# Weighted sums of eight decay heads: the value's high and low halves side by side in one weight block

## The reference, cut to what matters

```python
logit[t, s] = q_t . k_s / 8 + c[t] - c[s]          # c = cumulative sum of log forget gates, s <= t
p = softmax(logit)
attn = einsum('bhqk,bkhd->bqhd', p, v)              # per head: (512 x 512) x (512 x 64)
sgu = zu * (w_s @ layer_norm(zv) + b_s)             # z = gelu(...), split into zu, zv
merged = concat([rms_norm(attn), rms_norm(sgu)])
x = x + merged @ w_out
```

## Time and profile before

| | us |
|---|---|
| median of 3 runs | 1293.28 (1293.07 to 1293.45) |
| the profiled execution's own time | 1292.43 |
| its span | 1290.7 |
| PE busy | 1282.1 (99%) |
| DVE busy | 912.7 (71%) |
| ACT busy | 611.1 (47%) |
| POOL busy | 467.4 (36%) |

### The profile page before, as it was taken

How to read it: one execution, slowest core, us unless ns; L and a number is a source line. 1 busy time by engine, 2 the same in 40 slices (tenths; PEclk the granted TensorE clock), 3 DMA queues, 4 the chain that set the end, 5 groups by cost and what they waited for, 6 DMA issues and landing times.

```text
span 1290.7 us, 18190 instructions
## 1 busy us (share of the span) xinstructions
PE 1282.1 (99%) x6986; PEld 1095.9 (85%) x6986; DVE 912.7 (71%) x1284; ACT 611.1 (47%) x1007; POOL 467.4 (36%) x208
## 2 busy tenths in 40 slices
PE   9999999999999999999999999999999999999998
PEld 7787888898888888888889888898879999998886
DVE  7999826799283366666498685577989999985442
ACT  5223323335352466656654445578564444453223
POOL 2544544555434442452555343324420000015441
PEclk9999999999999999999999999999999999999999
DMA  4333333233832422326143346442323233223331
GB/s 165 98 98 106 116 96 99 66 98 115 293 97 83 133 64 82 83 63 216 49 147 115 116 152 167 124 115 99 98 69 128 99 110 120 99 94 103 114 98 66
DMA packets 48019, 143.66 MB, mean 111 GB/s; under 512 B 6048, under 2 KB 6048, under 8 KB 47040
## 3 DMA queue, kind: packets, MB, share of 16 engines
q1 hardware_dynamic: 43984, 129.88, 32.5%
q10 hardware_dynamic: 3952, 12.64, 2.7%
HBM read 121.46 MB, written 10.49 MB: 102 GB/s over the span
## 4 chain that ended last, share of the span: by engine, by line
PE 95%; DVE 2%; ACT 1%; issue 1%; DMA 0%; POOL 0%; SPq 0%; POOLq 0%; ACTq 0%
PE bank L2151 30%; PE bank L2153 30%; PE bank L2152 30%; PE bank L2389 2%; PE bank L2378 1%; PE bank L2379 1%; DMA x<-x_in 0%; POOL w_lo L714 0%; PE bank L2532 0%; PE bank L2533 0%; ACT pool_xg L822 0%; DVE zv L1884 0%; PE bank L2706 0%; ACT f_prob_t L1016 0%; DVE zu L1851 0%
## 5 line engine op out<-in xcount | busy, mean ns | idle before, releaser
L714 POOL TENSOR_TENSOR w_lo<-raw,w_hi 128x1024 fp32r<-128x1024 f32 (+1 forms) x146 | 372.8, 2558 | 518.6 <-ACT w_hi L782 518.5
L782 ACT ACTIVATE w_hi<-raw 128x1024 fp32r<-128x1024 f32 x149 | 156.1, 1053 | 176.1 <-PE bank L2153 93.5
L759 POOL TENSOR_TENSOR w_lo<-raw,w_hi 128x1024 fp32r<-128x1024 f32 x22 | 53.8, 2449 | 262.9 <-DVE w_lo L2008 204.5
L2151 PE MATMUL bank<-pool_xg,w_hi 128*128 128x512 f32 x248 | 98.6, 398 | 0.2 <-POOL w_lo L714 0.2
L2152 PE MATMUL bank<-pool_xg,w_hi 128*128 128x512 f32 x248 | 98.1, 396 | 0.0
L2153 PE MATMUL bank<-pool_xg,w_lo 128*128 128x512 f32 x248 | 98.1, 395 | 0.0
L2151 PE MATMUL bank<-right,w_hi 128*128 128x256 f32 x336 | 94.4, 281 | 0.0
L2153 PE MATMUL bank<-right,w_lo 128*128 128x256 f32 x336 | 94.1, 280 | 0.0
L2152 PE MATMUL bank<-right,w_hi 128*128 128x256 f32 x336 | 94.0, 280 | 0.0
L2090 DVE TENSOR_TENSOR act<-acts,act 128x512 fp32r<-128x512 f32 x22 | 47.6, 2167 | 51.0 <-ACT act L1249 51.0
L2151 PE MATMUL bank<-y_hi,w_hi 128*128 128x512 f32 (+1 forms) x216 | 81.0, 375 | 0.0
(11 more groups left out here) (469 smaller groups left out, 3726.2 us busy)
## 6 DMA issues: line engine op xcount, KB each, us to landing
raw<-stream SPq DMA_DIRECT2D x187, 512.0 KB, 3.5
raw_x<-stream SPq DMA_DIRECT2D x18, 512.0 KB, 4.7
xg_spill<-mla_xg ACTq DMA_DIRECT2D x2, 2048.0 KB, 12.0
rope_q<-turned_hl SPq DMA_DIRECT2D x64, 64.0 KB, 2.5
zx<-xg_spill SPq DMA_DIRECT2D x2, 1536.0 KB, 9.3
stacked<-fq SPq DMA_DIRECT2D x24, 128.0 KB
stacked<-fk SPq DMA_DIRECT2D x24, 128.0 KB
x<-x_in SPq DMA_DIRECT2D x4, 512.0 KB, 6.4
```

The source lines that it names most:

```text
L714: pool.tensor_tensor(w_lo[:, j % RING, 0:width], raw[:, j % RAW, 0:width], plain(w_hi[:, j % RING, 0:width]), ALU.subtract).then_inc(tile_ ...
L759: pool.tensor_tensor(w_lo[:, s, 0:D], raw[:, d % RAW, 0:D], plain(w_hi[:, s, 0:D]), ALU.subtract).then_inc(tile_lo, 1)
L782: act.activation(w_hi[:, t % RING, 0:width], raw[:, t % RAW, 0:width], ACT.Copy).then_inc(tile_hi, 1)
L2151: pe.matmul(target, a_hi, b_hi, start=start, stop=False)
```

## The change

It does five things.

1. The values are stored as `fv[P, NB, head, 2, 64]`: for every head the 64 high columns and the 64 low columns form one weight block of 128. A weighted sum is then two matmuls per key block (times the high and the low part of the probabilities) where three stood. Rows 0 to 63 of bank 5 hold the high values' sum, rows 64 to 127 the low values' sum.
2. ACT copies rows 64 to 127 to `low_half` for every head (`copy_low_half`), and DVE adds rows 0 to 63 of the bank to it, where it copied 64 rows before.
3. ACT's list in the heads is changed: casts of weight tiles 20, 21, 22, 23 stand in heads 4, 5, 7, 7 (before 4, 4, 5, 7); `attn_high(1)` is in head 5 instead of 4; the last evacuation of z is in two halves (`last_gates`), of which one goes to the end of head 5; the fourth `zvn_hi` goes to head 6. DVE's `attn_low(1)` goes from head 4 to the end of head 5.
4. PE counts `gates_halved` after the first fill of head 5.
5. DVE's scaling of a bank in `add_attention` counts `attn_taken`, and PE's branch transposes and later products wait for that instead of for the addition to x.

```diff
@@ values
-        fv_hi, fv_lo = (place(48 + 8 * i, f"fv_{i}", [P, NB, D_ATTN], f32r) for i in range(2))
+        fv = place(48, "fv", [P, NB, FOX_HEADS, 2, FOX_D], f32r)
+        low_half = place(155, "low_half", [FOX_D, S])
@@ ACT
+            def last_gates(part):
+                if part == 0:
+                    act.wait_ge(gates_halved, GATES_BEFORE + 1)
+                else:
+                    act.wait_ge(tile_used, MIXED["z", 7] + 1)
+                for b in range(2 * part, 2 * part + 2):
+                    act.activation(zu[:, b, QUARTER:], bank[6 + b // 2][:, QUARTER * (b % 2):QUARTER * (b % 2 + 1)], ACT.Copy,
+                                   scale=inv_t[:, b:b + 1]).then_inc(z_evac, 1)
+            def copy_low_half(h):
+                act.wait_ge(fox.weighted, h + 1)
+                if h:
+                    act.wait_ge(fox.out, h)
+                act.activation(low_half[:], bank[5][FOX_D:P, :], ACT.Copy).then_inc(low_half_copied, 1)
...
-                for i in ((12, 13), (14, 15), (16, 17), (18, 19), (20, 21), (22,), (), (23,))[h]:
+                for i in ((12, 13), (14, 15), (16, 17), (18, 19), (20,), (21,), (), (22, 23))[h]:
                     split_mix(i)
@@ DVE
-                if h in (2, 4):
-                    attn_low(h // 2 - 1)
+                if h == 2:
+                    attn_low(0)
+                if h == 5:
+                    attn_low(1)
                 dve.wait_ge(fox.weighted, h + 1)
-                dve.tensor_copy(attn[rows, h // 2, :], bank[5][rows, :]).then_inc(fox.out, 1)
+                dve.wait_ge(low_half_copied, HALVES_BEFORE + h + 1)
+                dve.tensor_tensor(attn[rows, h // 2, :], bank[5][0:FOX_D, :], low_half[:], ALU.add).then_inc(fox.out, 1)
@@ PE
-                    last = three(bank[5][:, P * b:S], fv_hi[:, b, a], fv_lo[:, b, a], f_prob_t_hi[:, r], f_prob_t_lo[:, r],
-                                 b == 0, b == NB - 1)
+                    v = fv[:, b, h, :, :].rearrange("p a d -> p (a d)")
+                    pe.matmul(bank[5][:, P * b:S], v, f_prob_t_hi[:, r], start=b == 0, stop=False)
+                    last = pe.matmul(bank[5][:, P * b:S], v, f_prob_t_lo[:, r], start=False, stop=b == NB - 1)
...
-                    pe.wait_ge(attn_added, 2)
+                    pe.wait_ge(attn_taken, TAKEN_ATTN + 2)
```

More of the change, by code:

```diff
@@ L460, in build @@
         v_summed, fv_hi_done, fv_lo_done = sem("v_summed"), sem("fv_hi_done"), sem("fv_lo_done")
+        low_half_copied, HALVES_BEFORE = lat_mean, 2
+        gates_halved, GATES_BEFORE = rope_k_summed, 1
+        attn_taken, TAKEN_ATTN = lat_inv, 2
         gate_abs_ready, gate_log, log_f_ready = sem("gate_abs_ready"), sem("gate_log"), sem("log_f_ready")
@@ L1123, in _ @@
                     act.wait_ge(v_summed, b + 1)
-                act.activation(fv_hi[:, b, :], bank[V_BANK[b]][:], ACT.Copy, scale=inv_t[:, b:b + 1]).then_inc(fv_hi_done, 1)
+                act.activation(fv[:, b, :, 0, :], by_head(bank[V_BANK[b]][:]), ACT.Copy, scale=inv_t[:, b:b + 1]).then_inc(fv_hi_done, 1)
             split_mix(11)
@@ L1136, in attn_square, with zvn_high @@
                 act.activation(attn_sq[:, pair, :], attn[:, pair, :], ACT.Square).then_inc(attn_squared, 1)
+            def zvn_high(b):
+                act.wait_ge(zvn_ready, b + 1)
+                act.activation(zvn_hi[:, b, :], zv[:, b, :], ACT.Copy).then_inc(zvn_hi_done, 1)
+            def last_gates(part):
[11 more added lines that the diff above has]
+                act.activation(low_half[:], bank[5][FOX_D:P, :], ACT.Copy).then_inc(low_half_copied, 1)
             qk_high(2)
@@ L1144, in _ @@
                     qk_high(3)
-                if h in (2, 4, 6):
+                if h in (2, 4):
                     sgu_evacuate(h // 2)
+                if h == 6:
+                    last_gates(1)
+                if h == 5:
+                    attn_high(1)
                 if h == FOX_HEADS - 1:
@@ L1156, in _ @@
                     qk_high(h + 4)
-                if h in (2, 4):
-                    attn_high(h // 2 - 1)
-                for i in ((12, 13), (14, 15), (16, 17), (18, 19), (20, 21), (22,), (), (23,))[h]:
+                if h == 4:
+                    copy_low_half(h)
+                elif h == 2:
+                    attn_high(0)
+                for i in ((12, 13), (14, 15), (16, 17), (18, 19), (20,), (21,), (), (22, 23))[h]:
                     split_mix(i)
@@ L1162, in _ @@
                     qk_high(h + 4)
+                if h == FOX_HEADS - 2:
+                    zvn_high(NB - 1)
+                if h < FOX_HEADS - 1 and h != 4:
+                    copy_low_half(h)
                 if h == 2:
@@ L1168, in _ @@
                 if h == 5:
-                    for b in range(NB):
-                        act.wait_ge(zvn_ready, b + 1)
-                        act.activation(zvn_hi[:, b, :], zv[:, b, :], ACT.Copy).then_inc(zvn_hi_done, 1)
+                    last_gates(0)
+                    for b in range(NB - 1):
+                        zvn_high(b)
             act.wait_ge(head_stacked[1], 8 * 16 * (FOX_HEADS // 2))
@@ L1852, in gate_groups, with square_sum @@
                                              col("b_s", g), mine, ALU.add, ALU.mult).then_inc(sgu_gated, 1)
+            def square_sum(pair):
+                dve.wait_ge(attn_squared, pair + 1)
+                return dve.tensor_tensor(attn_sqsum[:], attn_sq[:, 0, :] if pair == 1 else attn_sqsum[:], attn_sq[:, pair, :], ALU.add)
             qk_evacuate(2)
@@ L1940, in add_attention @@
                     t = mixed[:, k % 2, :]
-                    settle(dve.tensor_tensor(t, bank[ATTN_BANK[k]][:], attn_inv[:], ALU.mult))
+                    dve.tensor_tensor(t, bank[ATTN_BANK[k]][:], attn_inv[:], ALU.mult).then_inc(attn_taken, 1)
+                    dve.wait_ge(attn_taken, TAKEN_ATTN + k + 1)
                     dve.tensor_tensor(x[:, k, :], t, x[:, k, :], ALU.add).then_inc(attn_added, 1)
@@ L2468, in sgu_tile @@
                     last.then_inc(tile_used, 1)
+                return last
             pe.wait_ge(n.x_ready, 6)
@@ L2571, in fill @@
                 elif h < 6:
-                    sgu_tile(h + 2, range(2 * part, 2 * part + 2))
+                    done = sgu_tile(h + 2, range(2 * part, 2 * part + 2))
+                    if h == 5 and part == 0:
+                        done.then_inc(gates_halved, 1)
                 elif h == 6 and part == 0:
@@ L2632, in _ @@
                 if m < 6:
-                    pe.wait_ge(attn_added, m + 3)
+                    pe.wait_ge(attn_taken, TAKEN_ATTN + m + 3)
                 for c in range(SC):
```

11 lines of the change are left out of this document (5 added, 6 removed).

## The result

The changed kernel took 1298.01 us (median of 8 runs) where the kernel before took 1293.26: a ratio of 1.0034, interval 1.0025 to 1.0044. Measured again it was 1.0026 (1.0016 to 1.0036). It is slower, by 0.26 to 0.34%; forecast were 1294.6 us and a range up to 1296.4. One of the 8 runs took 4070.06 us; the ratio leaves it out. The profiled execution took 1298.0 (before: 1292.43), its span is 1296.3. From here on, times of day are those of the kernel that is named.

The account below looks back on a forecast made before the run. PE bounds the kernel, except from head 5's end to the mean, where the chain is mostly DVE and ACT. -3.1 + 2.75 + 1.55 - 0.1 + 0.2 = +1.3 us gave 1294.6 us; bounds 1293.0 to 1295.9, 8-in-10 range 1289.6 to 1296.4.

Parts of the forecast that it names:

- The matmuls removed: Weighted sums of heads 0 to 4: one pass of three less, 0.62 us each, 3.1 us gained.
- The copies in heads 0 to 4: ACT's copy in heads 0 to 4, near 0.60 us each, fits into ACT's idle time: cost 0.
- The end of head 5: Layer norm: POOL's low parts and DVE's steps alternate; head 7's transposes 2.75 us later (bounds 0 to 4).
- the step behind it: Head 6's first low part (878.25) to head 7's transposes: 5.85 us, so they start at 884.1, not 881.35.
- Ahead of the mean: Head 7's transposes to the mean: 14.0 us where it was 12.45, 1.55 us lost (bounds 0.6 to 2.4).
- Mean to branch: From the mean to the branch transposes: forecast -0.1 us against 12.24 before.
- attn_taken and the reload of x: Branch transposes' wait: at most 0.1 us gained; later reload, felt at first feed-forward tiles: 0.2 us lost (0 to 0.5).
- The slower rival: Behind the branch, POOL holds DVE's additions to x, delaying feed-forward operands: 1.8 us more, 1296.4 us; chance 0.15.
- parts 3 to 5: Losses: end of head 5, 0 to 4; transposes to mean, 0.6 to 2.4; reload, 0 to 0.5; `attn_taken` gain 0.1.

Follow-up runs that it names:

- both fills: Changed kernel plus unused products of ones by ones on TensorE, 16 in head 6 and 8 ahead of the mean: 1293.51 us, ratio 1.0008.
- POOL's order: Changed kernel, but POOL makes the low part of tile 21 behind the third `zvn_lo`: 1291.95 us, ratio 0.9994.
- attn(1) back: Changed kernel with `attn_high(1)` and `attn_low(1)` in head 4 again: 1294.55 us, ratio 1.0014.
- the moves alone: Kernel before with only tile casts 20 to 23, `attn_high(1)` and `attn_low(1)` moved as in the change: 1299.63 us, ratio 1.0045.
- both edits: Changed kernel with POOL's low part of tile 21 after the third `zvn_lo`, and `attn_high(1)` and `attn_low(1)` in head 4: 1291.83 us, ratio 0.9991.
- fill in head 6: Changed kernel plus 16 unused products on TensorE in head 6, none ahead of the mean: 1295.28 us, ratio 1.0013; executed again, 1294.61 us.

## Why the prediction was wrong

- **The matmuls removed: right.** -3.18 against -3.1; a third of 1.86 is what a pass is worth. By the figures of the Trainium skill that the prediction names ("TensorE: Matmul & The Clock Gate", "Back-to-back issue gap"), the same 20 matmuls would have been worth an estimated 1.6 to 2.6; the measurement decides against them here.
- **The copies in heads 0 to 4: right.** 0.59 us each; no stand of PE up to head 5.
- **The end of head 5: right in its mechanism, in the order of its steps and in its time.** POOL went first after DVE's second step, then they took turns. Head 6's first low part was forecast at 878.25 and came at 878.3. With the clock kept up (both fills) T5 to T7 is 20.79, +2.65; forecast was +2.75.
- **What failed is the step behind it: "Head 7's transposes start at 878.25 + 5.85 = 884.1".** It takes PE to be early, so that only DVE's way counts. The prediction itself let PE stand for 3 to 4 us there, and did not ask what its clock does then. At 1.2 GHz the product behind the stand took 4.96 us instead of 2.88, and PE became the later one: DVE had the probabilities ready at 882.3, PE came at 883.90. That is the 1.7 by which the term was too small (1.0 in the repeat).
- **Ahead of the mean: right.** 14.06 against 14.0.
- **Mean to branch: the same omission.** The prediction had PE stand "some 2 us ahead of the mean" and gave the 12 us of matmuls behind it their old length. They took 1.46 longer. Against the kernel with both fills the two falls cost (22.62 - 20.79) + (13.70 - 12.16) = 3.37 us in the profiled execution. Without them the net of +4.35 is +0.98, by the side of the +1.3 that was forecast; the kernel with both fills has +1.01.
- **attn_taken and the reload of x: right within 0.2.** The shift does not grow behind the branch. The slower rival (delayed additions) named the right side with the wrong mechanism: its extra 1.8 us were to come in the additions, and nothing came there.
- **The range.** The bounds given with parts 3 to 5 add up to 1290.7 to 1297.1, not to the 1293.0 to 1295.9 that the prediction states; even 1297.1 is below the 1298.01 measured, for no bound had the clock in it.
- **The median.** The profiled execution of before lay some 0.8 below its median, that of the changed kernel at its own, and the latter came to the heads 1.25 late. This is the scatter of the untouched part, and neither kernel's property; it accounts for the remaining 0.4 us of the 3.4 between forecast and median. Measured again, the ratio was 1.0026.

What stays open is what decides in a given run whether the clock falls behind a stand of 2 us. In the trace it did in five profiled executions (changed twice, POOL's order, attn(1) back, the moves alone, there behind 1.84 us), and not in three with the same 2.0 us (both edits, fill in head 6 twice). Both kinds have the same work in the same order there, and the clocks of the single runs say that it is not the kernel: POOL's order has the lower clock in 8 runs of 11, both edits and the fill in head 6 in 6 of 11. What differs between such runs is not shown. That the stand is needed is: with work put into it, none of 22 runs has the lower clock.

## What to carry to other kernels

A stand of TensorE has two prices: its own length, and the matmuls that run at half clock behind it. Where a forecast has TensorE wait for some microseconds on a path that it otherwise bounds, add the second price (here some 1.5 us for each 3.41 us at 1.2 GHz behind the mean), and look whether the work behind the stand is then later than the engine that caused it. Before an operation is moved on one engine, look at who follows it in order on another: here ACT's cast of another tile let POOL start a low part of 2.7 us inside DVE's layer norm, and DVE's steps waited for it. And look at more than one run before you say that a kernel has or has not a fall of the clock: the profiled execution is one draw, and the mean granted clock of every run is there to be counted.

## What the runs showed of the hardware that was not expected

- Useless matmuls made the kernel faster: 24 of them, in two stands, took the ratio from 1.0034 and 1.0026 (two measurements) to 1.0008, and the runs with a lower clock from 16 of 16 to 0 of 11.
- Stands of 1.8 to 2.4 us were followed by half clock in some executions of a kernel and not in others: the lower clock is in 8 of 11 runs with POOL's order (stand of 2.04 us), and in 9 of 11 with attn(1) back (2.38 and 2.05 us). The same stand of 4.04 us gave 6.83 us of it once and 3.41 us another time.
- The prediction had expected this, from one row: with three DVE operations of two SBUF inputs queued against POOL's low parts, the two engines took turns: 2.89, 1.77 and 1.75 us instead of 0.70, 0.70 and 0.75. Neither went twice in a row while the other was queued. The Trainium skill ("SBUF — State Buffer", "Who interferes with whom") has the exclusion, and these rows agree; the taking of turns is what they add.
